# Second feed-forward block and differential attention in one program block, with both norms between them taken tile by tile

## The reference

```python
x = x + mla(h, ...)                       # o.reshape(B, S, 1024) @ w_o
h = rms_norm(x, norm_ffn[1])
x = x + (silu(h @ w_gate) * (h @ w_up)) @ w_down      # 1024 -> 2816 -> 1024
x = rms_norm(x, norm_final)               # replaces x
h = rmsnorm(x, norm_mix_2[0])             # norm of the normed x
q, k, v = split(h @ w_in)                 # 1024 -> 3072
```

## Time and profile before

| | us |
|---|---|
| median of three executions | 1599.43 |
| lowest and highest | 1598.54, 1601.93 |
| the profiled execution | 1601.18 |
| its span, first to last instruction | 1599.4 |
| TensorE busy in it | 1510.6 |
| mean granted clock of TensorE | 0.973 |

### The profile page before, as it was taken

How to read it: one execution, slowest core, us unless ns; L and a number is a source line. 1 busy time by engine, 2 the same in 40 slices (tenths; PEclk the granted TensorE clock), 3 DMA queues, 4 the chain that set the end, 5 groups by cost and what they waited for, 6 DMA issues and landing times. The chain is left out here.

```text
span 1599.4 us, 18954 instructions
## 1 busy us (share of the span) xinstructions
PE 1510.6 (94%) x7353; PEld 1243.5 (78%) x7353; DVE 779.6 (49%) x926; ACT 673.4 (42%) x856; POOL 76.9 (5%) x57
## 2 busy tenths in 40 slices
PE   8999999999999999999999996999879579999996
PEld 7888888888886788888888885888558458888885
DVE  6433332232575334333332126344872568888884
ACT  5332223112455434232232124334861268777783
POOL 0000000000000000000000000000220012211110
PEclk9999999999999999999999998999999789999998
DMA  6222222323230112222322322232000789999993
GB/s 238 78 81 105 105 83 101 106 79 118 73 112 1 67 58 101 105 82 101 105 93 92 106 79 73 102 105 79 27 1 0 278 318 381 388 379 386 386 390 83
DMA packets 36018, 225.69 MB, mean 141 GB/s; under 512 B 5207, under 2 KB 5463, under 8 KB 11632
## 3 DMA queue, kind: packets, MB, share of 16 engines
q1 hardware_dynamic: 31200, 211.52, 35.0%
q0 software_dynamic: 4608, 13.22, 3.5%
q10 hardware_dynamic: 144, 0.03, 0.0%
HBM read 214.68 MB, written 13.63 MB: 143 GB/s over the span
## 5 line engine op out<-in xcount | busy, mean ns | idle before, releaser
L245 DVE TENSOR_TENSOR WL<-raw,WH 128x2048 fp32r<-128x2048 f32 x93 | 213.9, 2300 | 439.2 <-ACT WH L240 439.2
L250 PE MATMUL PS<-AH,WL 128*128 128x512 f32 (+1 forms) x768 | 286.5, 373 | 4.3 <-DVE AL L394 4.3
L251 PE MATMUL PS<-AL,WH 128*128 128x512 f32 (+1 forms) x768 | 285.8, 372 | 0.0
L252 PE MATMUL PS<-AH,WH 128*128 128x512 f32 (+1 forms) x768 | 285.8, 372 | 0.0
L240 ACT ACTIVATE WH<-raw 128x2048 fp32r<-128x2048 f32 x93 | 177.5, 1909 | 246.9 <-PE PS L252 246.9
L2387 DVE TENSOR_TENSOR WEL<-eraw,WEH 128x2048 fp32r<-128x2048 f32 x96 | 216.7, 2287 | 17.1 <-ACT WEH L2325 17.1
L2325 ACT ACTIVATE WEH<-eraw 128x2048 fp32r<-128x2048 f32 x96 | 181.6, 1912 | 19.8 <-PE PS L252 18.8
L250 PEld LDWEIGHTS PS<-AH,WL 128*128 128x128 f32 x768 | 145.4, 189 | 29.7 <-DVE AL L394 4.5
L251 PEld LDWEIGHTS PS<-AL,WH 128*128 128x128 f32 x768 | 145.4, 189 | 25.1
L252 PEld LDWEIGHTS PS<-AH,WH 128*128 128x128 f32 x768 | 145.3, 189 | 24.7
L250 PE MATMUL PS<-WH,AL 128*128 128x512 f32 (+2 forms) x416 | 156.2, 375 | 4.6 <-DVE WL L245 2.2
(11 more groups left out here) (318 smaller groups left out, 2104.6 us busy)
## 6 DMA issues: line engine op xcount, KB each, us to landing
eraw<-experts SPq DMA_DIRECT2D x96, 1024.0 KB, 11.2
raw<-stream SPq DMA_DIRECT2D x94, 1024.0 KB, 4.8
moe_rows<-moe_rows_g SPq DMA_DIRECT2D x5, 512.0 KB, 14.2
X<-x SPq DMA_DIRECT2D x4, 512.0 KB, 5.9
out<-X SPq DMA_DIRECT2D x1, 2048.0 KB, 20.1
ffn_row<-rows SPq DMA_DIRECT2D x2, 512.0 KB, 9.3
final_row<-rows SPq DMA_DIRECT2D x2, 512.0 KB, 5.8
cst<-consts SPq DMA_DIRECT2D x1, 733.5 KB, 13.7
```

Of the source, the lines that this page charges most:

```text
L245: dve.tensor_tensor(WL[:, u % SLOTS, :], raw[:, u % SLOTS, :], WH[:, u % SLOTS, :].bitcast(F32), ALU.subtract).then_inc(unit_lo, 1)
L250: pe.matmul(acc, lhs_lo, rhs_hi, start=start, stop=False)
L251: pe.matmul(acc, lhs_hi, rhs_lo, start=False, stop=False)
L252: return pe.matmul(acc, lhs_hi, rhs_hi, start=False, stop=stop)
```

## The change

There are four parts.

1. The second feed-forward block leaves through `down_by_tiles` too, and the program block goes on into `da_in`. The final norm (semaphores `w`) and the norm before attention (`v`) are done per tile: add, square, root, invert, scale in place, square, root, invert, scale with the gain row into `da_rows_g`, transpose, halves. A new transfer brings the gain row (`da_mix_row`). QKV block 0 runs in the order of the tiles, with the last two transposes inside it. `normalize`, `final_norm`, `project_pe` and `project_add` go.
2. `down_by_tiles`, which the first feed-forward block uses as well, makes each of its two transposes one group of products later.
3. The output of latent attention is turned and split tile by tile instead of by column block.
4. The banks of the QKV blocks are exchanged (block 0 needs 4 to 7 first), the tiles come in `ORDER`, the first scores wait for the last transposes' copies instead of the last V copies, and the transfer of `lam` is issued later.

```diff
         def down_by_tiles(...):
...
             unit_into(a, ORDER[2])
+            unit_into(a, ORDER[3]).then_inc(unit_used, 1)
             turn_tile(pe, leave.sems, 0, ORDER[0], leave.rows_g)
-            unit_into(a, ORDER[3]).then_inc(unit_used, 1)
+            unit_into(b, ORDER[2]).then_inc(leave.made, 1)
             turn_tile(pe, leave.sems, 1, ORDER[1], leave.rows_g)
-            unit_into(b, ORDER[2]).then_inc(leave.made, 1)
             unit_into(b, ORDER[3]).then_inc(unit_used, 1)
...
                     for t in range(T):
                         for c in range(C):
-                            mm = pe.transpose(PS[:, c, t * P:(t + 1) * P], O[:, t, c * P:(c + 1) * P], ident)
-                            if t == T - 1:
-                                mm.then_inc(turned, 1)
+                            mm = pe.transpose(PS[:, 2 * t + c // 4, (c % 4) * P:(c % 4 + 1) * P],
+                                              O[:, t, c * P:(c + 1) * P], ident)
+                        mm.then_inc(turned, 1)
...
-                    for c in range(C):
-                        act.wait_ge(turned, c + 1)
-                        act.activation(AH[:, c, :], PS[:, c, :], ACT.Copy).then_inc(o_hi, 1)
+                    for t in range(T):
+                        act.wait_ge(turned, t + 1)
+                        act.activation(AH[:, :, t * P:(t + 1) * P], tile_banks(t), ACT.Copy).then_inc(o_hi, 1)
...
+                    def load_row(sp):
+                        sp.wait_ge(unit_used, U_DA - 4)
+                        sp.dma_start(mix_row[:, :], rows[6:7, :].broadcast_to([P, D])).then_inc(mix_row_here, 16)
...
             @block.sync
             def _(sp):
+                for u in range(U_DA + 2, U_DA + 6):
+                    load_unit(sp, u)
+                sp.wait_ge(w.gained, T)
+                sp.wait_ge(unit_used, U_DA)
                 sp.dma_start(lam[:, :, :].rearrange("p a n -> p (a n)"),
                              lams.broadcast_to([P, 256])).then_inc(lam_here, 16)
...
+                pe.wait_ge(v.lo, 2)
+                pe.wait_ge(unit_lo, U_DA + 1)
+                part_into(0, 0, 0)
+                part_into(0, 0, 1)
+                pe.wait_ge(unit_lo, U_DA + 2)
+                part_into(0, 1, 0).then_inc(made, 1)
+                turn_tile(pe, v, 2, ORDER[2], rows_g)
+                part_into(0, 1, 1).then_inc(made, 1)
+                pe.wait_ge(v.lo, 3)
+                part_into(0, 0, 2)
+                turn_tile(pe, v, 3, ORDER[3], rows_g)
+                part_into(0, 1, 2).then_inc(made, 1)
+                pe.wait_ge(v.lo, 4)
+                part_into(0, 0, 3).then_inc(unit_used, 1)
+                part_into(0, 1, 3).then_inc(unit_used, 1)
...
+                def finish(n):
+                    t = ORDER[n]
+                    invert_tile(dve, w, n, t)
+                    dve.scalar_tensor_tensor(X[:, t, :], X[:, t, :], rstd[:, t:t + 1], final_row[:, :], ALU.mult,
+                                             ALU.mult).then_inc(w.gained, 1)
...
-                    if q == 0:
-                        pe.wait_ge(qk_here[h % 2], 5 + h // 2)
                     if i < 2:
-                        pe.wait_ge(v_here, 22 + 2 * i)
+                        pe.wait_ge(qk_here[0], 7 + i)
+                        pe.wait_ge(qk_here[1], 7 + i)
```

More of the change, by code:

```diff
@@ L273, in _ @@
                 dve.wait_ge(inverted, 1)
[L276 to L318, removed]
-                    for c in range(C):
-                        act.wait_ge(turned, c + 1)
[L321 to L340, removed]
-                    for t in range(T):
-                        pe.wait_ge(scaled, t + 1)
-                        for c in range(C):
-                            mm = pe.transpose(PS[:, c, t * P:(t + 1) * P], xs[:, t, c * P:(c + 1) * P], ident)
-                            if t == T - 1:
-                                mm.then_inc(turned, 1)
-            return scaled, turned, lo
@@ L1339, in mla_out_and_second_swiglu @@
             f = norm_sems("n3")
-            with nc.Block() as block:
+            w = norm_sems("nf")
+            v = norm_sems("n4")
+            v.added = w.gained
+            down_made = sem("f1_tile_made")
+            mix_row_here = sem("da_mix_row_here")
+            with nc.Block() as block, ExitStack() as later:
                 def unit_into(pe, d, t):
@@ L1387, in mla_out_and_second_swiglu @@
                     silu = sb("f1silu", [P, 2, S], F32, tmp)
+                    with ExitStack() as late:
+                        mix_row = sb("da_mix_row", [P, D], where=late)
+                        mix_rows_g = sb("da_rows_g", [P, 2, D], where=late)
                     with ExitStack() as early:
@@ L1517, in da_in @@
+        def da_in(block, held, w, v, down_made, mix_row_here, mix_row, rows_g, QK, V, QT, KT, square, ls, unsloped, lam_ready, emptied, qk_emptied):
             made = sem("da_made")
@@ L1529, in da_in, with bank @@
             lam = sb("lam", [P, 4, 64], where=held)
-            gained = final_norm(block)
-            _, _, turned_lo = normalize(block, "n4", QK[:, :, 0:D], "mix2", (U_DA, U_DA + 1), QK[:, 0:2, D:2 * D],
-                                     lambda engine, t: engine.wait_ge(gained, t + 1), act_tiles=range(T))
+            def bank(b, n):
+                return (0 if b in (1, 3) else 4) + n
             def home(n):
@@ L1549, in _, with part_into @@
             def _(pe):
-                for b in range(6):
+                def part_into(b, part, n):
+                    t = ORDER[n]
+                    u = U_DA + 2 * b + part
+                    for k in range(4):
+                        c = 4 * part + k
+                        cols = slice(k * 512, (k + 1) * 512)
+                        mm = product(pe, PS[:, bank(b, n), :], AH[:, c, t * P:(t + 1) * P], AL[:, c, t * P:(t + 1) * P],
+                                     WH[:, u % SLOTS, cols], WL[:, u % SLOTS, cols], c == 0, c == C - 1)
+                    return mm
```

261 lines of the change are left out of this document (125 added, 136 removed).

## The result

| | before | changed |
|---|---|---|
| median of twelve executions, us | 1601.38 | 1591.80 |
| lowest and highest | 1598.54, 1602.70 | 1586.18, 1595.20 |
| the profiled execution (span) | 1601.18 (1599.4) | 1586.74 (1584.7) |
| mean granted clock of TensorE in it | 0.973 | 0.979 |

The ratio is 0.9938, with a 95% interval of 0.9923 to 0.9952: 9.6 us faster. The forecast was 1589.8 with a range of 1587.0 to 1594.0, so the time came out 2.0 above it and inside the range. Beside the experiments the changed kernel was timed again, 1593.24 against 1601.89 (0.9941, 0.9921 to 0.9960).

The account below looks back on a forecast made before the run. TensorE was taken as the bound, busy 1510.6 of 1599.4 us. The sum 1601.18 - 11.0 + 2.8 - 1.5 + 0.1 - 2.0 + 0.8 = 1590.4, less 0.6, gave 1589.8, range 1587.0 to 1594.0.

Parts of the forecast that it names:

- The second seam: From second feed-forward block's unit a to QKV block 2: 73.0 us against 84.04, with waits 0.4, 2.0, 1.8; 11.0 less.
- The shared helper: Transposes of `down_by_tiles` one group later delay the first feed-forward block's followers, latent attention's products: 2.8 us more.
- The attention output: Latent attention's output turned by tiles: first product at about 551.1 instead of 552.56; 1.5 us less, 1.2 at least.
- Part 4: Exchanged QKV banks change no count; first scores wait for later copies, between 0 and 0.5 us, taken as 0.1 more.
- The clock: TensorE's low clock: first seam loses 1.0 instead of 3.0, so 2.0 us less; second seam loses 0.8 more.
- The first rival: No clock is lost at either seam after the change: 1588.0 us; chance 0.2.
- second clock rival: Each new group of waits brings the clock down; first seam keeps its 3.0, second loses 1.7 to 3.4: 1592.7 to 1594.4; chance 0.14.
- the last step, from the sum to the median: Profiled execution is 1.75 over the median of three, partly chance clock loss: 0.6 us taken off, 1590.4 to 1589.8.
- The slower rival: QKV block 0's first unit returns late, not made up; all 11 remaining waits of 1.8 stand, 20 us: 1608; chance 0.03.

Follow-up runs that it names:

- kernel with the first seam early: Against the changed kernel, only the first feed-forward block turns its tiles one group earlier again, as before the change; 1589.47 us, ratio 0.9920 to the kernel before.
- kernel with both seams early: Against the changed kernel, both feed-forward blocks turn their tiles one group earlier, as the helper did before the change; 1593.57 us, ratio 0.9955 to the kernel before.

## Why the prediction was right, and where it was off

**The second seam** was forecast at 73.0 and measured 73.47, in two profiles alike. The waits were to be 0.4, 2.0 and 1.8 and are 0.31, 2.07 and 1.84, each released as said; the rest, 0.4, is in terms too small to name. The durations came from the earlier trace rows, where the first seam does the same work; that is the likely reason why they fit.

**The shared helper** was forecast to cost 2.8. It does: 59.5 against 56.7, both without clock loss, and the early order put back in the second seam costs 3.9 where the list said 4.0.

**The attention output**: 1.5 forecast, 3.53 for 5.02 measured, and 1.5 again when undone. **Part 4**: from QKV block 2 to the first score it is 94.31 before and 94.32 after.

**The clock.** The forecast was 1.0 lost in the first seam and 0.8 in the second, as means over 0 to 3. Eight profiles have the changed lists in the first seam: five lose about 0.2, three 1.5 (59.1 to 59.7, and 61.0), 0.7 on average. In the five the low clock falls on the products ahead of the waits and costs next to nothing, as the prediction said. Eight have them in the second: four lose nothing (73.42 to 73.47) and four about 1.6 (75.05 to 75.62, the last with 0.6 of address in it), 0.8 on average. Of the seven that have both, six lose 1.5 or more in one seam or the other, none in both, and one, the first profile, in neither. One of the four with a low clock in the second seam, before and within it (the kernel with the first seam early):

```profile
962.50:965.20 2.70, 0.79 (x4) 0.35 (x4) 2.67 (x4) 2.21 (x2) 0.00 (x0) 1.00 0.00 0
965.20:968.60 3.40, 3.40 (x9) 2.65 (x10) 3.40 (x3) 2.22 (x4) 0.00 (x0) 0.50 0.75 253
```

Behind a wait as short as 2.07 the clock can fall, then, but it did so only in half the profiles, and it stayed up behind the 3.31 of the kernel with both seams early: the length of one wait doesn't decide. The first rival is what the first profile shows. The second is not what any shows, for no profile with the changed lists kept the 3.0 in the first seam. The rule that needs one longer idle gap, quoted in the prediction from the Trainium skill (TensorE: Matmul & The Clock Gate, the section on HAM oscillation), gives the first rival's 1588.0 and is contradicted here again, by the 2.07 with a low clock behind it. "By the page" in the prediction means this section's rule alone.

**What was off** is the last step, from the sum to the median. I took 0.6 off because the profiled execution lay 1.75 above the median of three. With twelve executions that median is 1601.38, and the profiled one is typical: the 0.6 was not there to take. The second size that was off is the low clock of the old first seam. It was counted at 3.0, half of 6.0 us; by the starts of the products (0.240 for 0.133) it is 2.7. And three profiles with the old order lose 2.7, 2.6 and 1.5, 2.3 on average, so the change gave back 1.6 there, not 2.0. With both put right and 73.47 for 73.0, the sum from 1601.18 is 1601.18 - 10.6 + 2.8 - 1.5 + 0.0 - 1.6 + 0.8 = 1591.1, against 1591.8 and, the second time, 1593.2 (beside 1601.9). The rest is within what the medians can tell. Two statements of the prediction don't follow from its own numbers: the range up to 1594.0 does not take in all of the second clock rival, which reaches 1594.4, and eleven waits of 1.8 on top of 1589.8 are 1609.6, not 1608.

That the two first profiles differ by 14.4, not 9.6, is chance, most of it of the same kind. The untouched stretch from the first score to the first expert product is 174.64 in one and 172.51 in the other, the first seam pays 2.7 to the clock in one and 0.2 in the other, and the first inputs land 0.4 later in one. The changed kernel's second profile is 6.6 later than its first, all but 0.9 of it by the clock.

The slower rival, a late weight unit that is never made up, did not occur: 94.32 from block 2 to the first score leaves no room for it.

## What to carry to other kernels

When a seam is taken tile by tile, lay out the list of each engine with measured durations before writing the order: every wait of the changed kernel, and the loss in the block that shares its helper, were in that list, and two of the waits went when the lists were reordered, with a weight split ahead of the low halves. Where executions differ by where the clock falls, judge a change of 1 to 4 us by distances between the same instructions in several traces, and take the base from more than three executions. Look at the start-to-start interval of equal matmuls in different stages: a difference of 3% may be an address.

## What the runs showed of the hardware that was not expected

- **Operand addresses.** An fp32r matmul of 128x512 starts 226.7 to 227.1 ns after the one before when both operands begin at 160 modulo 256 bytes in their partitions, and 232 to 234 ns on average when one of them begins at 224, 32 or 64: 3.5 us for 528 matmuls, shown in both directions; the one exception is `CTH`. Other equal addresses and what is behind it were not tried. `CTH` at 224 fits where it is the stationary operand (233) and not quite where it is the moving one (229), which stays unexplained; at 160 both are at 227 to 228.
- **The granted clock can fall behind waits of 2 to 3 us, and at different places in equal executions**: right behind the first wait of the first seam (415.2, price 0.2, since later waits take it back) or behind the last one (425.4, price 1.5). The same wait of the second seam left it up in four of eight profiles.
- **A faster TensorE met the transfers at once**: 7 ns less for each expert matmul gave 2.2 us of 8.5, and ScalarE's waits went from TensorE to the landing of weights.
